# A decoder step on one core: another order of the sample scores, the decay scans and the index-key gathers around a 31-round search

## What is computed

```python
h = rms_norm(x) @ w_in                    # one input projection, columns cut into parts
# A: sparse attention over the keys that an indexer selects
s = einsum('bthd,bsd->bths', iq, ik) * 64 ** -0.5
score = einsum('bths,bth->bts', relu(s), iw)       # causal positions only
idx = top_k(score, 256)                             # prompt: among 1024 keys, samples: 1025
a_out = softmax(q @ k[idx] + bias) @ v[idx]
# B: gated linear recurrence, 8 heads, state 64 x 64, in chunks
f = lb + (1 - lb) * sigmoid(h_f); g = log(f); b = cumsum(g)       # per chunk
o = (masked q k^T with decay exp(b_t - b_s)) @ v + (q exp(b)) @ S
S = exp(b_last) * S + (k exp(b_last - b))^T @ v
y = x + concat(a_out * silu(gate_a), rms_norm(o) * silu(gate_h)) @ w_out
```

## Time and profile before

| | us |
|---|---|
| median of 3 runs | 848.31 |
| lowest, highest | 847.95, 849.04 |
| profiled execution | 851.93 |
| its span, first to last instruction | 849.9 |
| TensorE busy | 800.7 (94%) |
| VectorE busy | 584.8 (69%) |
| ScalarE busy | 414.9 (49%) |
| GpSimd busy | 393.3 (46%) |

### The profile page before, as it was taken

How to read it: one execution, slowest core, us unless ns; L and a number is a source line. 1 busy time by engine, 2 the same in 40 slices (tenths; PEclk the granted TensorE clock), 3 DMA queues, 4 the chain that set the end, 5 groups by cost and what they waited for, 6 DMA issues and landing times.

```text
span 849.9 us, 18220 instructions
## 1 busy us (share of the span) xinstructions
PE 800.7 (94%) x6633; PEld 737.0 (87%) x6633; DVE 584.8 (69%) x1152; ACT 414.9 (49%) x1213; POOL 393.3 (46%) x575
## 2 busy tenths in 40 slices
PE   4999999997899999999999999978899998999998
PEld 3889888996899989999999999966777877898998
DVE  3645865989988999889996626696866467555111
ACT  6765763340554587558364735544545454422100
POOL 4343635308934395449667245238663337410500
PEclk9999999998999999999999999999999999999999
DMA  7211111301001212041204235396544644341422
GB/s 268 89 41 51 62 45 45 103 1 50 26 26 51 83 56 89 26 123 41 88 2 136 77 100 151 100 244 157 141 143 157 193 134 140 115 135 46 143 78 74
DMA packets 69180, 81.32 MB, mean 96 GB/s; under 512 B 20234, under 2 KB 55738, under 8 KB 68842
## 3 DMA queue, kind: packets, MB, share of 16 engines
q1 hardware_dynamic: 64410, 66.58, 25.3%
q0 software_dynamic: 4688, 13.64, 5.8%
HBM read 62.85 MB, written 17.34 MB: 94 GB/s over the span
## 4 chain that ended last, share of the span: by engine, by line
PE 56%; issue 14%; DVE 11%; DMA 10%; POOL 5%; ACT 3%; SPq 1%; DVEq 0%; POOLq 0%; ACTq 0%
PE psum L2150 17%; PE psum L1242 12%; PE psum L2147 7%; DMA index_keys_T<-in_cache_ikt,index_page_rows 7%; POOL w_low L522 3%; PE psum L1193 3%; DVE flag L1925 3%; PE psum L1211 3%; PE psum L2046 3%; DMA page_keys<-in_cache_kt 2%; DVE bit_kept L1939 2%; PE psum L1172 1%; PE psum L1178 1%; PE psum L1176 1%; PE psum L2031 1%
## 5 line engine op out<-in xcount | busy, mean ns | idle before, releaser
L2150 PE MATMUL psum<-w_high,xT_high 128*128 128x256 f32 x720 | 206.1, 286 | 10.4 <-POOL w_low L522 5.8
L2150 PE MATMUL psum<-w_low,xT_high 128*128 128x256 f32 x720 | 202.9, 282 | 0.0
L2150 PE MATMUL psum<-w_high,xT_low 128*128 128x256 f32 x720 | 202.8, 282 | 0.0
L1925 DVE TENSOR_SCALAR_CACHE_REDUCE flag<-scores,candidate 128x384 f16<-128x384 f32 (+2 forms) x192 | 181.7, 946 | 6.9
L522 POOL TENSOR_TENSOR w_low<-w_raw,w_high 128x256 fp32r<-128x256 f32 (+1 forms) x168 | 128.1, 801 | 62.0 <-ACT w_high L1595 52.2
L2150 PEld LDWEIGHTS psum<-w_high,xT_high 128*128 128x128 f32 x720 | 128.8, 179 | 14.0 <-POOL w_low L522 6.1
L2150 PEld LDWEIGHTS psum<-w_high,xT_low 128*128 128x128 f32 x720 | 128.8, 179 | 2.6
L2150 PEld LDWEIGHTS psum<-w_low,xT_high 128*128 128x128 f32 x720 | 128.8, 179 | 2.3
L2147 PE MATMUL psum<-xT_high,w_high 128*128 128x384 f32 (+3 forms) x312 | 102.3, 328 | 1.1 <-POOL w_low L522 1.1
L2147 PE MATMUL psum<-xT_high,w_low 128*128 128x384 f32 (+3 forms) x312 | 99.7, 319 | 0.0
L2147 PE MATMUL psum<-xT_low,w_high 128*128 128x384 f32 (+3 forms) x312 | 99.6, 319 | 0.0
(11 more groups left out here) (314 smaller groups left out, 1845.1 us busy)
## 6 DMA issues: line engine op xcount, KB each, us to landing
w_raw<-in_w_main SPq DMA_DIRECT2D x40, 512.0 KB, 4.1
x_rows<-in_x_prompt SPq DMA_DIRECT2D x8, 512.0 KB, 5.9
page_keys<-in_cache_kt SPq DMA_DIRECT2D x32, 128.0 KB, 3.2
page_keys<-in_cache_kt POOLq DMA_DIRECT2D x32, 128.0 KB, 3.9
page_values<-in_cache_v SPq DMA_DIRECT2D x32, 128.0 KB, 3.4
page_values<-in_cache_v POOLq DMA_DIRECT2D x32, 128.0 KB, 3.7
x_res<-in_x_prompt SPq DMA_DIRECT2D x32, 128.0 KB
out<-y_rows SPq DMA_DIRECT2D x32, 128.0 KB
```

Source lines behind the costliest of these rows:

```text
L1925: dve.tensor_scalar(JK[:, 0:w], sc, threshold(k), None, op, ALU.add, accum_out=CNT[:, k:k + 1]).then_inc(s["dve_chain"], 1)
L2150: last = pe.matmul(ps(BANK[n], w, rows(i)), x[:, k, row0(i):row0(i) + rows(i)], ww[:, sl, k, 0:w], start=first, stop=final)
```

## The change

Four edits in three engines' queues. (1) On GpSimd, three of the eight gathers of pair 1 go ahead of `split_w(2)` and three of pair 2 ahead of `split_w(3)`. (2) On GpSimd, the memsets ahead of `split_w(6)` wait for `sample_index_summed` (TensorE's products are in PSUM) instead of `sample_index_ready` (VectorE has copied them); TensorE takes over the wait for the copy, ahead of the first chunk, which writes these PSUM banks. (3) On VectorE, the copy of the sample scores moves from behind round 6 to behind round 2. (4) `scan(0)`, `scan(1)` and `scan(2)` stand behind rounds 6, 17 and 27 instead of 7, 18 and 28.

```diff
-            def load_index_keys(bp):
+            def load_index_keys(bp, g0, g1):
...
-                for g in range(NPG):
+                for g in range(g0, g1):
...
+            load_index_keys(1, 0, 3)
             split_w(gp, 2)
-            load_index_keys(1)
+            load_index_keys(1, 3, NPG)
+            load_index_keys(2, 0, 3)
             split_w(gp, 3)
-            load_index_keys(2)
-            load_index_keys(3)
+            load_index_keys(2, 3, NPG)
+            load_index_keys(3, 0, NPG)
...
-                    gp.wait_ge(s["sample_index_ready"], 1)
+                    gp.wait_ge(s["sample_index_summed"], 1)
...
-            rounds(0, 6)
+            rounds(0, 2)
             sample_scores()
-            rounds(6, 7)
+            rounds(2, 6)
             scan(0)
-            rounds(7, 18)
+            rounds(6, 17)
             scan(1)
-            rounds(18, 28)
+            rounds(17, 27)
             scan(2)
-            rounds(28, ROUNDS)
+            rounds(27, ROUNDS)
...
                 if kind == "intra":
+                    if n == 0:
+                        pe.wait_ge(s["sample_index_ready"], 1)
```

More of the change, by code:

```diff
@@ L1502, in _ @@
             link(gp.tensor_tensor(PGX[:, :], PGX[:, :], ROWN[:, :], ALU.add))
-            load_index_keys(0)
+            load_index_keys(0, 0, NPG)
             gp.wait_ge(s["const_in"], CONSTS_IN)
```

## The result

| | before | after |
|---|---|---|
| median, us | 848.66 (4 runs, 847.95 to 849.04) | 836.84 (4 runs, 834.43 to 837.77) |
| ratio | | 0.9857, 95% interval 0.9835 to 0.9879 |
| profiled execution, us | 851.93 | 837.77 |
| its span, us | 849.9 | 835.8 |

The change saves 11.8 us on the medians; 835.9 had been forecast. The profiled execution of before is not one of its four, that of after is.

The account below looks back on a forecast made before the run. TensorE bounds the kernel, losing 11.7 us between 200 and 225. Waits of 5.84 and 2.74 plus 2.9 of clock give 11.5, pair 1 adds 0.9: 848.3 - 12.4 = 835.9 us, own range 834.5 to 838.0, wider range 832.0 to 841.0.

Parts of the forecast that it names:

- the step: GpSimd's gathers: each costs 2.96 us on average, so three fewer behind the second split end 8.9 us earlier.
- the allowance of 1.0 us for the split: VectorE beside split_w(6): three tiny instructions, each held for half to all of one 0.7 us GpSimd instruction.
- Rival (b): split_w(6) locks VectorE out for the full 5.6 us; gain only 9.1 us, time 839.2; chance 0.12.
- the 5.84 us: TensorE's wait for w_low of unit 6 at 205.48, claimed to go with 18 us to spare.
- Pair 0: TensorE between 200 and 225 us: both waits go and the clock doesn't fall, 11.5 us gained.
- The clock term of 2.9: TensorE between 200 and 225 us: time lost at the lower clock after standstills, regained with both waits gone.
- Pair 1: Around scan(1), 13.6 us earlier at 280.4: two of TensorE's three waits for ScalarE go, 0.9 us gained.
- the 0.94 at the spill: Largest of TensorE's three waits for ScalarE in pair 1, 0.9 us; tied to a spill moving with TensorE, stays.
- Pairs 2 and 3: From scan(2) on: nothing more gained; masks begin at 406.2, and slack of some 11 us covers pair 3's first chunk.
- rival (d): The change doesn't do what it says: memsets wait for something else or the tail returns the gain; 848, chance 0.04.

Follow-up runs that it names:

- the page numbers: The changed kernel with SyncE's 32 page numbers loaded one unit earlier in its queue: 836.29 us, ratio 0.9867.
- the edit-4 kernel: The kernel before with only the scans moved, to behind rounds 6, 17 and 27, the copy still behind round 6: 845.49 us against 847.72.
- the kernel of both cures: The changed kernel with SyncE's page numbers a unit earlier and GpSimd waiting for its own last product ahead of the pair's split_w: 837.86 us, ratio 0.9875.

## Why the prediction was right, point by point

| step | predicted | measured |
|---|---|---|
| search begins | 136.5 | 136.65 |
| gathers end | 133.5 | 128.7 |
| `scan(0)` | 188.7 | 188.23 |
| memsets, end of `split_w(6)` | 172.7, 181.5 | 170.1, 181.5 |
| `k_decayed` of pair 0 | 211.4 | 210.24 |
| TensorE's first chunk | 213.6 | 213.99 |
| gain of pair 0 | 11.5 | 12.2 (from product to product) |
| `scan(1)` | 280.4 | 278.48 |
| gain of pair 1 | 0.9 | 1.3 (from there to the product near 437) |
| masks | 406.2 | 405.18 |

**Edit 1** held, but the gathers gained 13.8 us (the last one's start, 141.44 and 127.63), not 8.9. The term that was off is the step. Behind `split_w(3)` three steps fewer were worth 10.9 us (35.7 us from its first gather to its last, where it had been 46.6), 3.6 each instead of 2.96. The other 2.9 us came from ahead of it: the first gather of pair 2 doesn't wait for one of its own pair and follows 1.25 us behind the last of pair 1 (75.43, 76.68), where I had put a mean step of 2.96, and `split_w(3)` took 8.71 us instead of 9.34. It made no difference, because the scores were the later of the two, as stated.

**Edits 3 and 4** held, with the allowance of 1.0 us for the split: at 179.31 and 180.18 two tiny instructions took 0.83 and 0.65, together 1.1 more than their usual 0.23 and 0.17. Rival (b) did not come, and not by a chance of one execution: in all eleven traces in which `split_w(6)` lies there, no `bit_kept` beside it took over 0.83. Why this split spares it, while the same instruction was held 7.11 us a few rounds later, no run shows; the allowance had the right size without a reason that was tested.

**Edit 2** was described wrongly. Its heading credited it with the 5.84 us. The changed kernel without it keeps that gain, since the copy ends at 158 and the register loads at 170. The prediction had both numbers (158 and 172.7) and did not compare them. The sum was unharmed, because nothing was counted twice.

**Pair 0** held: both waits gone, the clock back. The clock term of 2.9 was a little small (11.7 - 8.6 is 3.1; of the 12.2 measured, some 3.4 are neither the two waits nor the 0.14 at the spill). The sum formed from two waits and a clock was right only as a whole: edits 2 and 3, each removing the first wait, showed that it returns at the second place while the scan is late.

**Pair 1**: the size was about right (the waits of 0.59 and 0.27 went, the 0.94 at the spill stayed as 0.80), one reason was wrong. GpSimd was not released by `scan(1)` but by the spill (11.27 us). The same wait of SyncE's stands behind the 0.80 that I had called tied to TensorE; it goes with the page numbers.

**Pairs 2 and 3** held: the masks moved as said, `scan(3)` waited 1.16 instead of 4.87, and the edit-4 kernel bore masks 4 us later than before without loss.

**14.1 or 11.8?** The spans of the profiled executions differ by 14.1 us, 13.3 of which were there by the product near 437, 1 us more than the 12.4 forecast. The medians say 11.8. Part of the difference is between executions of one kernel. In two stretches the kernel before had a clock of 0.97 where edit 3 alone, with the same code there, had 1.00. Before, then edit 3 alone:

```profile
550.00:600.00 50.00, 42.66 (x374) 33.78 (x372) 40.10 (x85) 23.76 (x39) 29.69 (x44) 0.97 0.74 192
700.00:750.00 50.00, 46.38 (x408) 42.38 (x408) 31.48 (x72) 20.83 (x54) 26.70 (x27) 0.97 0.42 133
```

```profile
550.00:600.00 50.00, 42.15 (x381) 32.86 (x382) 41.66 (x92) 23.98 (x37) 32.62 (x49) 1.00 0.73 189
700.00:750.00 50.00, 47.23 (x426) 43.61 (x426) 32.22 (x77) 18.59 (x53) 23.16 (x23) 1.00 0.40 124
```

0.03 of 100 us is at most 3 us; the profiled execution of before lay 3.3 us above its median. But this doesn't settle the comparison, since the changed kernel's profiled execution has 0.97 in two such stretches too (550 to 600 and 650 to 700). What sets it off in one execution and not in another stays open.

Another part may be a real loss behind 437. In each of the eight other kernels with more than one execution and a gain of 7 us or more from product to product, the median gained 1.1 to 3.7 us less than the distance, against the kernel before beside it (5.4 and 8.6 for edits 3 and 4, 9.5 and 12.1 without edit 2). By the ratios of the table it is 0.6 to 4.1 us less in seven of them and 0.5 more in the eighth, edit 1 alone; in three a loss ahead of the first product is in it. The kernel before came there to medians of 846.75 to 847.84; against those the changed kernel's 836.84 is 10 to 11 us. So it looks as if the last stages give back a part, which rival (d) had in it at full size. No run shows where. That the median came within 1 us of the forecast may then be luck in part, two errors that cancel: more gained up to 437, some of it lost behind.

## What to carry to other kernels

Where an engine waits at two places in a row, find out whether both hang on one late producer before adding up the waits: taking away the first alone (edits 2 and 3) only moved it to the second. Cost a set of edits by chains, each reader at the latest of its producers; a single edit pays by itself only if it moves the common start of the chains (the gathers, 8.1 of 12.2 us from product to product); edits 3 and 4, one for each chain, gain 8.6 together and 1.3 and 1.9 alone. To judge effects of 1 us, compare the distance between two products on the bounding engine's timeline, not total times that scatter by several us; but look at the total as well, since a gain in one stretch can be lost in a later one.

## What the runs showed of the hardware

**A VectorE instruction can be kept out for a whole run of GpSimd's.** In the changed kernel `bit_kept`, 0.23 us alone, took 7.11, 9.90 and 6.41 us. Each began at or among the `q_decayed` products and ended with the run, nine or more instructions on. A pause of 0.08 us lets it in: 0.90, and in the kernel of both cures 0.93, 0.91 and 0.91, each of the four ending in the pause. It is not always kept out: in the kernel without edit 2 the `bit_kept` at 391.47, at the same place in the same run without a pause, took 0.90. The six counts of each round, which also run beside GpSimd, kept their times (0.61 to 1.28 us by size).

The Trainium skill (SBUF — State Buffer, Who interferes with whom) says that a `tensor_scalar` may enter a mode that uses the shared ports and the form with an accumulator may not; the steady counts and the held `bit_kept` agree with it. It also says that the holder keeps the ports for its instruction; the three rows show more than that, since VectorE was kept out over nine or more instructions of GpSimd's. Why the `bit_kept` at 179.31, inside `split_w(6)`, and the one at 391.47 got in after 0.8 to 0.9 us is open.

**It can also reach TensorE:** 5.68 and 5.59 us for a scores product, 1.69 and 1.59 us of TensorE's time, in the profiled executions of two kernels whose edits lie 100 us further on. That the phase between the two engines decides it was not tested.

**The reverse:** a scan beside `split_w(6)` stretched the split from 5.53 to 7.51 us, and to 7.60 in the kernel with edit 1 alone.
